# A two-block model on one core: the first block's state space steps laid between half tiles of its input projection

## The chip, the core and the metric

The kernel runs on one core of a Trainium2 chip. The metric is the device time in microseconds of one execution, the median of three. The engines are TensorE (PE, with its weight loads as PEld), VectorE (DVE), ScalarE (ACT), GpSimd (POOL) and SyncE (SP); the last two mainly start transfers here. They run on their own and meet at semaphores.

## The reference

All in float32, 512 tokens of width 1024. The first block, cut to what the change touches:

```python
mod = (silu(c) @ w_ada + b_ada).reshape(6, 1024)      # shift, scale, gate, twice
h = rmsnorm(x) * (1 + scale_m) + shift_m
proj = h @ w_in                                       # pool 512 | z 1024 | xbc 1536 | dt 16
y_pool = pool_mixer(proj[:, :512])                    # trailing means of 2, 4, 8, 16 tokens, one 128x128 product a group
conv = silu(conv4(xbc) + conv_b)                      # xs 1024 | b 256 | c 256
dt = softplus(dt_raw + dt_bias); a = dt * -exp(a_log) # 16 heads
a_cs = cumsum(a within a chunk of 128)                # 4 chunks
decay = exp(where(causal, a_cs[l] - a_cs[s], -inf))   # 16 heads x 4 chunks, 128x128 each
y_diag = (c @ b.T * decay) @ (xs * dt)
states = b.T @ (exp(a_cs[-1] - a_cs) * xs * dt)       # scanned over the chunks to h_prev
y = y_diag + exp(a_cs) * (c @ h_prev) + xs * d_skip
y_ssd = rmsnorm(y * silu(z)) * ssd_norm
x = x + gate_m * (concat([y_pool, y_ssd]) @ w_out)    # 1536 -> 1024
h = rmsnorm(x) * (1 + scale_f) + shift_f              # goes to the query product of a top-k expert layer
```

Behind it come the expert layer and a second block (gated linear attention, an S5 layer, a feed-forward part), which the change leaves as they are. The S5 layer's parameter tables are made early, in the shadow of the first block's output and query products.

## The kernel before, in words

Activations lie feature major: 8 regions of 128 features x 512 tokens in one large SBUF tile, `arena`. A product of the projection is a 128x128 weight tile against 128x512 tokens; 8 of them (12 in the output product) fill one PSUM bank, an output tile. `STAGES` names the stages: "in" has 24 tiles (12 of xbc, 8 of z, 4 of pool), "out" 8, "query" 16.

Order is what the code of each engine says. `Turn` (L163) issues an instruction and waits for its own semaphore before the next one, unless the name begins with "~". Semaphores of many events are shared (`SHARED`), so events of one semaphore must come in the order of that table. `bank_free` counts banks copied out of PSUM, `unit_done` counts finished weight tiles, and SP reloads a ring of four weight slots after them.

- POOL's queue loads the constants, c, w16 (the weights of dt), x, then 48 rows of w_ada through 8 buffers; a buffer is reused when VectorE has reduced its row (`mod_done`) and when the constants are there (`alone`).
- VectorE reduces 16 rows (`mod_row`), takes the reciprocal of the root, modulates x (`modulated`, two operations a tile), reduces 32 more rows, runs 12 convolutions (one multiply, three multiply-adds each), waits for the four pool tiles, pools them, then makes softplus on 16 partitions x 512 tokens and a scan.
- TensorE sums squares (L1218), makes dt (L1243) and all 24 tiles (`stage_products`, L521), waits until all are copied out, transposes, makes the chunk states (L1281), and goes through the heads: a row of the head (L1292, a selector of 16 partitions against the scan), which VectorE subtracts from the column (`seg`), ScalarE turns into a decay by Relu and Exp (`dec_e`), VectorE masks (`mdec`), and TensorE multiplies (`ssd_diag`, L1235). Two buffers alternate. After 8 heads come three products with the states (L1300) and the transposes back (L1226); then the gate with Silu(z).
- After 16 heads: one square of everything, sum of squares, root, norm (`ymix`), the four pool products (L1319), and only then the output product (L502), which waits for `pool_out` and `ymix` at its start. VectorE then makes the S5 tables and adds the tiles to x; the tables' products stand behind output tiles 4 to 7 (`tables_after`). The second norm and modulation repeat the pattern of the first, and the query product follows.

## Time and profile before

| | |
|---|---|
| median of three runs | 3052.07 us (3051.73 to 3059.96) |
| profiled execution | 3057.77 us, span 3056.1 us |
| TensorE busy | 2762.0 us (90%) |
| VectorE, ScalarE, POOL busy | 1880.7, 912.5, 868.6 us |
| chain that ended last | 60% TensorE, 16% issue, 16% VectorE |
| mean granted TensorE clock | 0.95 |

How it is read: "busy" is the time in which an instruction runs, not time at its peak. The clock row is the granted share of 2.4 GHz, so 0.50 is the lower level of 1.2 GHz. "Idle before" an instruction belongs to the event that released it. A float32 product appears as two matrix instructions, a transpose as one. The first block up to its query product takes the first 562 us of the span.

### The profile page before, as it was taken

The numbers are of one execution on the slowest core, as the hardware profiler recorded it, in microseconds if no ns is written. First come the engines' busy times: TensorE is split into PE (matmuls) and PEld (weight loads), VectorE is DVE, ScalarE is ACT, GpSimd is POOL, SyncE is SP. The second block draws the span as 40 slices with busy tenths as digits, with TensorE's granted clock in tenths as the row PEclk, the third lists the DMA queues.
The fourth block names the chain that finished last, engine by engine and source line by source line (L and its number), as shares of the span: only waits on it lengthen the run. The fifth ranks groups of instructions, "written<-read, shape, count | busy, mean of one in ns | idle before, by whom it ended". The sixth has DMA issues, their size and how long they took to land.

```text
span 3056.1 us, 36105 instructions
## 1 busy us (share of the span) xinstructions
PE 2762.0 (90%) x12753; PEld 2143.8 (70%) x12753; DVE 1880.7 (62%) x3290; ACT 912.5 (30%) x1121; POOL 868.6 (28%) x547
## 2 busy tenths in 40 slices
PE   4993769799996779999999999999999899899997
PEld 1442434348995569999999988779767777578875
DVE  7606356668999978888788889761114744361442
ACT  1020111223335643232332322344223323322221
POOL 3000000014660023344444432134212124244442
PEclk8995569899999999999999999999999999899999
DMA  8420003343332379989989889622713442222221
GB/s 335 160 87 9 0 33 108 127 155 104 118 121 119 154 262 317 317 306 323 316 309 317 302 299 319 211 90 82 140 42 102 138 146 90 69 83 96 91 96 62
DMA packets 190240, 500.79 MB, mean 164 GB/s; under 512 B 30704, under 2 KB 79872, under 8 KB 188080
## 3 DMA queue, kind: packets, MB, share of 16 engines
q1 hardware_dynamic: 140528, 315.20, 31.2%
q0 software_dynamic: 49616, 184.42, 16.8%
q8 instruction: 47, 0.77, 0.1%
q14 instruction: 49, 0.40, 0.0%
HBM read 452.70 MB, written 46.86 MB: 163 GB/s over the span
## 4 chain that ended last, share of the span: by engine, by line
PE 60%; issue 16%; DVE 16%; POOL 4%; DMA 1%; DVEq 1%; ACT 1%; POOLq 0%; ACTq 0%; SPq 0%
PE psum L1388 17%; PE psum L1670 13%; PE psum L1379 11%; PE psum L502 6%; PE psum L521 5%; DVE arena L1715 5%; POOL l_r L802 4%; DVE arena L1718 2%; DVE arena L1722 1%; PE psum L1292 1%; PE psum L1235 1%; DVE arena L2049 1%; DVE arena L2046 1%; DVE arena L2047 1%; DVEq L1718 1%
## 5 line engine op out<-in xcount | busy, mean ns | idle before, releaser
L827 ACT ACTIVATE arena<-psum 128x512 f32 (+7 forms) x487 | 328.3, 686 | 1282.9 <-PE psum L1379 392.6
L1715 DVE TENSOR_TENSOR arena<-arena 128x384 f32<-128x384 f32 (+11 forms) x396 | 342.0, 867 | 526.8 <-ACT arena L827 301.9
L802 POOL TENSOR_TENSOR l_r<-arena,l_r 128x1024 fp32r<-128x1024 f32 x144 | 352.2, 2447 | 704.8 <-ACT l_r L477 704.8
L1388 PE MATMUL psum<-e_r,e_r 128*128 128x512 f32 x2304 | 542.0, 392 | 11.1 <-DVE e_r L1715 11.1
L1379 PE MATMUL psum<-e_r,e_r 128*128 128x384 f32 x2048 | 524.7, 337 | 11.6 <-POOL l_r L774 8.0
L1388 PEld LDWEIGHTS psum<-e_r,e_r 128*128 128x128 f32 x2304 | 433.2, 189 | 99.7 <-issue 9.1
L1379 PEld LDWEIGHTS psum<-e_r,e_r 128*128 128x128 f32 x2048 | 369.7, 188 | 25.8 <-POOL l_r L774 15.0
L827 ACT ACTIVATE e_r<-arena 128x1024 fp32r<-128x1024 f32 x256 | 270.2, 1057 | 360.2 <-PE psum L1388 340.0
L1379 PE MATMUL psum<-e_r,l_r 128*128 128x384 f32 x1024 | 343.6, 336 | 0.0
L786 POOL DMA_INDIRECT arena<-in_down_rows,arena x128 | 162.8, 1272 | 424.4 <-DMA scratch_gates<-arena 179.7
L786 POOL DMA_INDIRECT arena<-in_up,arena x128 | 163.5, 1278 | 278.3 <-DVE arena L2145 144.3
L1715 DVE TENSOR_TENSOR e_r<-arena,e_r 128x384 fp32r<-128x384 f32 (+1 forms) x264 | 220.2, 877 | 13.4 <-ACT e_r L827 11.8
L502 PE MATMUL psum<-arena 128*128 128x512 f32 x448 | 199.8, 603 | 15.5 <-DVE arena L1719 14.6
L1722 DVE SCALAR_TENSOR_TENSOR arena<-arena 128x1024 f32<-128x1024 f32 (+5 forms) x157 | 191.5, 1221 | 24.7 <-ACT arena L827 15.2
L462 PE MATMUL psum<-p_r,l_r 128*128 128x264 f32 (+1 forms) x1024 | 196.1, 328 | 6.3 <-POOL l_r L802 5.2
L1670 PE MATMUL psum<-l_r,l_r 128*128 128x512 f32 x768 | 184.6, 401 | 11.0 <-DVE l_r L1722 11.0
L1379 PEld LDWEIGHTS psum<-e_r,l_r 128*128 128x128 f32 x1024 | 192.1, 188 | 0.0
L477 ACT ACTIVATE l_r<-arena 128x1024 fp32r<-128x1024 f32 x144 | 152.4, 1058 | 131.2 <-PE psum L1670 93.2
L1670 PE MATMUL psum<-f_r,l_r 128*128 128x512 f32 x768 | 181.8, 397 | 0.0
L1670 PEld LDWEIGHTS psum<-l_r,l_r 128*128 128x128 f32 x768 | 146.1, 191 | 49.6 <-issue 10.9
L1518 PE MATMUL psum<-p_r,l_r 128*128 128x512 f32 x576 | 179.2, 404 | 1.6 <-ACT arena L827 1.6
L462 PEld LDWEIGHTS psum<-p_r,l_r 128*128 128x128 f32 x1024 | 161.9, 190 | 25.2 <-issue 7.1
(222 smaller groups left out, 3435.7 us busy)
## 6 DMA issues: line engine op xcount, KB each, us to landing
arena<-in_down SPq DMA_DIRECT2D x128, 512.0 KB, 4.3
arena<-in_up SPq DMA_DIRECT2D x128, 512.0 KB, 6.6
arena<-in_w_ada POOLq DMA_DIRECT2D x48, 512.0 KB, 8.6
scratch_gates<-arena SPq DMA_DIRECT2D x12, 2048.0 KB, 6.3
arena<-scratch_gates SPq DMA_DIRECT2D x32, 768.0 KB, 9.8
arena<-in_w_in SPq DMA_DIRECT2D x44, 512.0 KB, 3.5
arena<-in_w_query SPq DMA_DIRECT2D x16, 512.0 KB, 3.5
arena<-in_w_glu SPq DMA_DIRECT2D x16, 512.0 KB, 3.5
```

What stands on the lines that cost most here:

```text
L462: last = nc.tensor.matmul(bank(2 * j + h, cw), rr(w_ + k * P, P, "l"), x_[:, c0:c0 + cw], start=(p == 0 and k == 0 and n == 0), stop=(p == ...
L502: last = nc.tensor.matmul(bank(2 * (v % 4)), wslot(s, kt)[:, k, :], rhs(k, 0, w), start=(k == 0), stop=(k == kt - 1))
L521: last = nc.tensor.matmul(bank(2 * j + h, cw), wslot(s, kt)[:, k, :], rhs(p * kt + k, c0, cw), start=(p == 0 and k == 0), stop=(p == parts ...
L786: pool.indirect_dma_start(reg(GATH + g % NGATH * 1024, 1024), None, rows_d if kind == "d" else rows_u, bass.IndirectOffsetOnAxis(reg(at_, ...
L802: nc.gpsimd.tensor_tensor(rr(lo, 1024, "l"), reg(RING + q % NSLOT * SLOT, 1024), rr(hi, 1024, "l").bitcast(F32), ALU.subtract).then_inc(S[ ...
L827: do(sc.activation(out, in_, f, **kw), sem)
L1379: last = mm(bank(b, TD), w__, rr(b_ + k * TD, TD), start=(k == 0 and n == 0), stop=(k == 7 and n == 2))
L1388: last = mm(bank(2 * tt_ + hf), rr(w__ + tt_ * P, P), rr(x__ + hf * 512, 512), start=(first and n == 0), stop=(final and n == 2))
L1518: last = mm(bank(v % 2), rr(w__ + k * P, P, "l"), x_[:, META:T2], start=(k == 0 and n == 0), stop=(k == 7 and n == 2))
L1670: last = mm(bank(2 * (t % 4)), rr(w__ + k * P, P, "l"), x_[:, META:T2], start=(p == 0 and k == 0 and n == 0), stop=(p == parts - 1 and k = ...
L1715: do(v.tensor_tensor(out, a, b, op), sem)
L1722: do(v.scalar_tensor_tensor(out, a, s, b, op0, op1), sem)
```

## The change

It rewrites the order of the first block.

- Loads: c and 8 rows of w_ada go first on POOL's queue and the constants behind them; SP loads x in 8 parts, and w_in's first four tiles after 6 rows are reduced. The order of w_in is now xbc, pool, z. X is overwritten by the chunk states and loaded again (`x_again`) before the output tiles are added to it.
- First norm: squares tile by tile, sum of squares tile by tile; VectorE multiplies by the reciprocal root (`scaled_x`), ScalarE applies scale and shift (`modulated`), and tile 0 starts with the first of them. The second norm (`xr2`, `h2_ready`) is built alike.
- Time steps token major: dt is 32 products with tokens on the output's partitions, softplus and the rest are on 128 x 64, the cumulative sum is a product with the causal matrix (`acol`), and a head's row is four products of a broadcast column of `a_col` with the same matrix (`ssd_row`). Selector and scan are gone. ScalarE takes the difference from the column as the bias of Relu, so VectorE's subtraction is gone.
- Convolutions: ScalarE makes the first tap while it copies; VectorE runs them between rows of w_ada, during the projection.
- Tiles 12 to 23 of the projection are cut into halves of four products (`in_half`), which stand between the state space steps. The pool tiles are pooled and multiplied among the first eight heads. Tiles 16 to 23 share bank 6.
- The first four products of output tiles 0 to 3 (the pool rows) are issued before the state space rows are ready; their other eight follow after the norm.

The diff, cut to its core ("..." where lines are left out):

```diff
-HST = H
-BTOK = H + 3072
+HST = X
+BTOK = X + 3072
...
+            if first:
+                for k in range(KT):
+                    sp.dma_start(reg(X + k * T, T), io["xT"][k * P:(k + 1) * P, :]).then_inc(S[f"x_in{k}"], 16)
+                sp.wait_ge(S["mod_done"], S.base("mod_done") + 6)
...
+        def in_bank(v):
+            return 2 * (v % 4) if v < 12 else 6 + v % 2 if v < 16 else 6
+        def in_free(v):
+            return v + 1 if v < 12 else 16 if v < 14 else v + 3 if v <= 16 else v + 4
+        def far_bank(v):
+            return (6, 2, 4, 0)[v % 4]
...
+            pool.dma_start(reg(CACT, D), io["c"].broadcast_to([P, D])).then_inc(S["c_in"], 16)
+            for m in range(8):
+                pool.dma_start(reg(ADA + m * 1024, 1024), io["w_ada"][m]).then_inc(S[f"ada_in{m}"], 16)
             pool.dma_start(cst[:, :], io["consts"]).then_inc(S["small_in"], 16)
...
+            def modulated(shift0, sem, done):
+                for k in range(KT):
+                    wait(sem, k + 1)
+                    h = reg(H + k * T, T)
+                    act_(h, h, ACT.Identity, "~" + done, scale=gsc[:, k:k + 1], bias=mod[:, shift0 + k:shift0 + k + 1])
...
+            def decay(h):
+                wait("row_mm", h + 1)
+                if h >= 2:
+                    wait("diag_mm", h - 1)
+                m = MB_ + (h % 2) * T
+                for c in range(NCH):
+                    act_(reg(m + c * P, P), bank(h % 2)[:, c * P:(c + 1) * P], ACT.Relu, FREE if c < 3 else None, scale=-1.0,
+                         bias=acol[:, c * 16 + h:c * 16 + h + 1])
+                act_(reg(m, T), reg(m, T), ACT.Exp, "~dec_e", scale=-1.0)
...
+            def ssd_row(h):
+                if h >= 2:
+                    w_("dec_e", h - 1)
+                for c in range(NCH):
+                    last = mm(bank(h % 2)[:, c * P:(c + 1) * P], bc(a_col[:, c * 16 + h:c * 16 + h + 1], [P, P]), causal,
+                              start=True, stop=True)
...
-            stage_products(pe, "in", tok(H))
-            drained("in")
+            for v in range(1, 12):
+                in_part(pe, v, 0, KT)
+                if v == 4:
+                    w_("a_col", 1)
...
+            ssd_xs(0)
+            ssd_xs(1)
+            in_half(13, 0)
+            ssd_xs(2)
+            ssd_xs(3)
+            in_half(13, 1)
+            w_("btok", 2)
+            ssd_state(0)
+            in_half(14, 0)
...
+            for h in range(8):
+                ssd_row(h)
+                in_half(16 + h // 2, h % 2)
+                if h:
+                    ssd_diag(h - 1)
+                if h >= 4:
+                    pool_mix(h - 4)
...
+            for v in range(4):
+                far_tile(pe, "out", v, YMIX, 4, 12, (lambda k: w_("ymix", k - 3)) if v == 0 else None)
+            for v in range(4, 8):
+                far_tile(pe, "out", v, YMIX, 0, 12)
+                tables_after("out", v)
...
-            for n in range(16):
+            for n in range(12):
+                mod_row(n)
+            wait("small_in", 48)
+            tt(g_sq, pr("norm_final"), pr("norm_final"), ALU.mult)
+            ts(g_sq, g_sq, EPS, None, ALU.add, sem="g_sq")
+            wait("rt1", 1)
+            do(v.reciprocal(RS[:, 0:T], RS[:, 0:T]))
+            for n in range(12, 16):
                 mod_row(n)
```

How the instructions stand now. First VectorE at the end of the first norm; L1744 and L1930 reduce a row of w_ada, L1754 and L1939 are the reciprocal. Before:

```order
L1744 ISA arena,mod<-arena 128x1024 [waits ada_in7,mod_done]
L1744 ISA mod 128x1
L1715 TENSOR_TENSOR mod<-mod,par 128x16 [waits mod_done]
L1722 SCALAR_TENSOR_TENSOR gsc<-mod,par 128x8 [waits dve_own]
L1754 RECIPROCAL rs<-rs 128x512 [waits act_events,dve_own]
```

And after:

```order
L1904 TENSOR_TENSOR gsc<-par 128x8 [waits small_in,mod_done]
L1908 TENSOR_SCALAR gsc<-gsc 128x8 [waits dve_own]
L1939 RECIPROCAL rs<-rs 128x512 [waits act_events,g_sq]
L1930 ISA arena,mod<-arena 128x1024 [waits ada_in4,dve_own]
L1930 ISA mod 128x1
L1930 ISA arena,mod<-arena 128x1024 [waits ada_in5,mod_done]
L1930 ISA mod 128x1
L1930 ISA arena,mod<-arena 128x1024 [waits ada_in6,mod_done]
L1930 ISA mod 128x1
L1930 ISA arena,mod<-arena 128x1024 [waits ada_in7,mod_done]
L1930 ISA mod 128x1
L1904 TENSOR_TENSOR mod<-mod,par 128x16 [waits mod_done]
```

The reciprocal has moved ahead of four rows, and it now stands behind the wait for the constants (`small_in`).

TensorE in the first heads; L1292 and L1342 make a head's row, L1235 and L1333 are the masked products, L519 is a half tile. Before:

```order
L1281 MATMUL psum<-arena 128x512 x6
L1292 MATMUL psum<-rs,arena 128x512 x2
L1235 MATMUL psum<-arena 128x64 x4
L1292 MATMUL psum<-rs,arena 128x512
L1235 MATMUL psum<-arena 128x64 x4
L1292 MATMUL psum<-rs,arena 128x512
```

And after:

```order
L519 MATMUL psum<-arena 128x512 x8
L1342 MATMUL psum<-cst,small 128x128 x4
L519 MATMUL psum<-arena 128x512 x4
L1342 MATMUL psum<-cst,small 128x128 x4
L519 MATMUL psum<-arena 128x512 x4
L1333 MATMUL psum<-arena 128x64 x4
L1342 MATMUL psum<-cst,small 128x128 x4
L519 MATMUL psum<-arena 128x512 x4
```

Between a head's row and its masked products now stand two half tiles and the next row, where one row stood.

TensorE at the start of the output product; L502 and L534 are its tiles, L1218 and L1386 sums of squares, L1319 the pool products, L1300 and L1364 the products with the states. Before:

```order
L1300 MATMUL psum<-arena 128x512 x3
L1226 MATMUL psum<-cst,arena 128x128 x16
L1218 MATMUL psum<-arena,cst 128x512 x8
L1319 MATMUL psum<-arena 128x512 x4
L502 MATMUL psum<-arena 128x512 x60
L1226 MATMUL psum<-cst,arena 128x128 x8
```

And after:

```order
L1364 MATMUL psum<-arena 128x512 x3
L534 MATMUL psum<-arena 128x512 x4
L1323 MATMUL psum<-cst,arena 128x128 x12
L534 MATMUL psum<-arena 128x512 x4
L1323 MATMUL psum<-cst,arena 128x128 x4
L1386 MATMUL psum<-arena,cst 128x512 x4
L534 MATMUL psum<-arena 128x512 x4
L1386 MATMUL psum<-arena,cst 128x512 x4
L534 MATMUL psum<-arena 128x512 x48
L1323 MATMUL psum<-cst,arena 128x128 x8
```

Four groups of four output products have moved ahead of and between the transposes and the sum of squares, and the pool products are gone from here.

## Rows read from the trace of the kernel before

**Rows 1.** Windows: span, length, busy of PE PEld DVE ACT POOL, granted clock, DMA share, GB/s

```profile
4.00:48.00 44.00, 9.40 (x16) 3.88 (x16) 27.33 (x43) 8.04 (x6) 13.26 (x25) 0.84 1.02 401
...
62.66:227.70 165.04, 165.04 (x385) 72.87 (x384) 64.25 (x105) 25.55 (x38) 11.30 (x21) 1.00 0.40 147
227.70:262.06 34.36, 0.03 (x2) 0.03 (x1) 29.02 (x48) 3.34 (x5) 0.00 (x0) 0.56 0.07 23
262.06:299.68 37.62, 22.62 (x78) 13.81 (x78) 18.06 (x28) 2.35 (x7) 0.00 (x0) 0.64 0.00 0
299.68:413.37 113.69, 82.78 (x204) 45.54 (x204) 41.45 (x62) 20.15 (x32) 0.00 (x0) 0.50 0.00 0
413.37:443.71 30.34, 15.66 (x25) 5.96 (x25) 12.01 (x14) 7.04 (x5) 1.07 (x2) 0.67 0.19 72
443.71:533.67 89.96, 89.96 (x240) 41.55 (x240) 60.02 (x98) 12.51 (x20) 4.45 (x7) 0.98 0.27 91
533.67:562.15 28.48, 9.25 (x17) 3.73 (x17) 12.29 (x18) 6.45 (x5) 0.50 (x1) 0.72 0.05 16
...
227.70:232.00 4.30, 0.02 (x1) 0.00 (x0) 3.31 (x6) 0.60 (x1) 0.00 (x0) 1.00 0.53 183
232.00:236.00 4.00, 0.00 (x0) 0.00 (x0) 3.73 (x9) 0.00 (x0) 0.00 (x0) 0.50 0.00 0
```

**Rows 2.** Timeline of TensorE: start, busy us, engine, line, operation, shapes [idle before <-releaser]

```profile
22.57 9.40 PE L1218 MATMUL psum<-arena,cst 128*128 128x512 f32 x16 [22.57 <-ACT arena L827]
53.51 9.21 PE L1243 MATMUL psum<-arena,w 128*16 128x512 f32 x16 [21.54 <-DVE arena L1719]
...
310.19 1.97 PE L1235 MATMUL psum<-arena 128*128 128x64 f32 x8 [1.38 <-DVE arena L1715]
312.09 2.07 PE L1292 MATMUL psum<-rs,arena 16*128 16x512 f32 x2
...
496.95 1.04 PE L1226 MATMUL psum<-cst,arena 128*128 128x128 f32 x8
...
562.15 16.15 PE L502 MATMUL psum<-arena 128*128 128x512 f32 x32 [14.57 <-DVE arena L1719]
...
693.59 6.64 PE L1368 MATMUL psum<-arena 128*128 128x128 f32 x58
```

**Rows 3.** Timeline of VectorE, prologue to output stage

```profile
13.43 0.17 DVE L1715 TENSOR_TENSOR gsc<-par 128x8 f32<-128x8 f32 x1 [10.87 <-DMA w<-in_w]
...
20.17 1.23 DVE L1744 CUSTOM_DVE_ANT_0 arena<-arena 128x1024 f32<-128x1024 f32 x1 [6.37 <-DMA arena<-in_w_ada]
...
41.01 3.35 DVE L1754 RECIPROCAL rs<-rs 128x512 f32<-128x512 f32 x1
...
100.03 2.33 DVE L1722 SCALAR_TENSOR_TENSOR arena<-arena,par 128x512 f32<-128x512 f32 x3
...
314.20 0.69 DVE L1715 TENSOR_TENSOR arena<-psum,small 128x512 f32<-128x512 f32 x1 [4.06 <-PE psum L1292]
...
457.24 2.56 DVE L1715 TENSOR_TENSOR arena<-arena 128x64 f32<-128x64 f32 x10
...
473.04 1.41 DVE L1722 SCALAR_TENSOR_TENSOR arena<-psum,mod,arena 128x512 f32<-128x512 f32 x2
...
487.52 5.00 DVE L1715 TENSOR_TENSOR arena<-arena 128x1024 f32<-128x1024 f32 x4
```

**Rows 4.** Timeline of ScalarE, in the same stages

```profile
201.16 9.01 ACT L827 ACTIVATE arena<-arena,par 128x512 f32<-128x512 f32 x12 [0.18 <-ACT arena L827]
...
309.63 1.29 ACT L827 ACTIVATE arena<-arena 128x512 f32<-128x512 f32 x2 [4.06 <-DVE arena L1715]
...
413.37 3.62 ACT L827 ACTIVATE arena<-arena 128x4096 f32<-128x4096 f32 x1 [18.85 <-DVE arena L1715]
...
428.57 0.60 ACT L827 ACTIVATE rs<-psum 128x512 f32<-128x512 f32 x1
436.03 1.28 ACT L827 ACT_TABLE_LOAD   x1 [6.86 <-DMA arena<-in_s5a]
```

## What I predicted, before the changed kernel ran

> **What bounds the kernel now.** The page's busy shares say TensorE is at 90%, but the windows by stage show where it isn't. I read these first [rows 1]. From 62.66 us TensorE is full for 165.04 us (24 tiles of the input projection; each product is two of the 385 instructions of 0.43 us, so 0.86 us for a product of 128x512 and 6.88 us for a tile). Then it stands still for 34.36 us (pooling and time steps on VectorE), is busy 22.62 of 37.62 us, 82.78 of 113.69 us (the 16 heads) and 15.66 of 30.34 us, and all of this at a granted clock of 0.50 to 0.67, half of it at the 1.2 GHz level. The output product is full again (89.96 us), the second norm costs 28.48 us, then the query product starts at 562.15. The timelines show why [rows 2 to 4]: one head is a ring. TensorE makes a row (2.07 us at half clock), VectorE subtracts (0.69, after waiting 4.06), ScalarE does Relu and Exp (1.29), VectorE masks, TensorE multiplies. No engine has other work in it. So the path to 562.15 is: prologue, projection, vector work alone, ring, norm, output, norm. What comes after is not touched.
>
> **What the change does to the sum.** Zero is the span's start; I follow TensorE in the new order, at full clock where it has work.
>
> Prologue. c and the first 8 rows of w_ada now go first on POOL's queue, x on SP's, w_in only after 6 modulation rows. DMA moves 401 GB/s [rows 1]. Before, w16 had landed at 13.43 [rows 3]; 1.74 MB of POOL's and as much of SP's were ahead, 8.7 us, so 4.7 us go to start and completion. By that, w_ada row 0 lands at about 10 instead of 20.17 [rows 3], but the constants, behind 4.7 MB on POOL's queue and 2.1 MB of x, land at about 24.5 instead of 13.4. Two things are queued behind that: TensorE's sum of squares and POOL's loads of w_ada from row 8 on. The first takes 9.40 us [rows 2], to 34, its root 0.60 [rows 4], the table being loaded already. Row 8 needs issue, transfer and completion, so it comes at about 30, and the next every 1.3 us (0.52 MB at 401 GB/s). VectorE needs 1.28 us a row [rows 3], so 12 rows end at 35.5, the reciprocal (3.35, [rows 3]) at 39.4, four rows at 44.5, the first product with x at 45.6 (0.69 to 0.72), ScalarE's scale and shift at 46.4 (0.75, [rows 4]). Tile 0 starts there; its 8 products find TensorE as long idle as the 8 of the time steps did at 53.51, and take their 9.2 us [rows 2]: 55.7. The time steps become 32 products of 16 columns. No row has this form. Bounds: 0.13 us each (transposes, 1.04 for 8) and 0.29 us (9.21 for 32, the old cost); I take the 0.229 of 128-column products (6.64 for 29, [rows 2]), since each loads 128x128 weights: 7.3 us. **Tile 1 starts at 63.0** instead of 69.5.
>
> Tiles 1 to 12. 11 x 6.88 and two small products: 138.9. VectorE in that time: rows 16 to 25, softplus now on 128x64 instead of 16x512 (24 operations of about 0.26, [rows 3], 6 us), then 12 times a convolution (2.33, [rows 3]) and two rows: ends 142.6, 2.4 us after the last tile is copied out; its Silu 143.5. Tile 12 waits for the last copy-out (0.9) and ends at 146.7, so it covers this, with 3 us to spare. The pooling and softplus stretch of 34.36 us is gone from the path.
>
> Transposes, states. 8 + 32 transposes and 8 products of 128 columns 7.1 us, 6 products of 512 columns 5.2, six halves of tiles 13 to 15 20.6, two gaps of 0.95 where a half tile does not stand between two transposed chunks: 34.8, so **181.5**. The halves cover xdt, xdte and the state updates (0.7 to 2.8 us each against 3.44).
>
> Heads. A head now costs TensorE 0.92 (four row products at 0.229) + 3.44 (half tile) + 0.92 (four mask products). The first eight, with four pool products of 0.86, are 44.7 us: 226.2. The mask of a head is wanted 7.8 us after its row. ScalarE needs four Relu of 128 columns, which no row shows: between 0.15 us each (a quarter of a 128x512 from PSUM, 0.60) and 0.60. A square of 4096 columns took 3.62, so 512 columns beyond the first cost 0.45 and 0.15 is fixed [rows 4]: 0.15 + 0.11, and I take 0.3. With Exp that is 1.9 us, at worst 3.1; the mask adds 0.7. At both ends it is hidden; if the cover were gone it would cost about 3 us a head. The bank of tiles 16 to 23 is one, so each waits for its predecessor's copy-out, 0.8 us against 1.9 of other products: hidden. The second eight with 8 halves, 3 state products, 16 transposes and two stalls (1.6 for the last token row, 2.0 for the last mask) are 51.4: **277.6**.
>
> To the output product. 3 state products 2.6, four first halves of output tiles (pool rows) 13.7, transposes 2.1, sum of squares 6.9: 302.9, with the sum ending at 299.4. Root, reciprocal and first scaled row then take 5.1 us (0.6 + 3.35 + 0.75 and hand-overs), of which 3.44 is hidden: 304.5. Second halves 27.5: 332.0, tile 4: 342.3. x is loaded a second time after 280 on POOL's queue, 2.1 MB, which by the count above takes 10 us, and is wanted at 339; S5's parameters stand behind it on that queue, but are issued only at 299.4.
>
> What is late next: VectorE. Its tables start when S5's parameters land, 8.8 us after the sum of squares (Exp's table load at 436.03 against the root at 428.57 after its own 1.28 load, [rows 4]), at 310. To the first output tile it took 29.3 us (443.7 to 473.04, [rows 1, 3]), 2.9 for four output tiles, 3.75 for the first table product (three of the four in 5.00): 346.0. Before, the output product was 53 us in by then; now TensorE has done half of it ahead and is at 342.3. It waits 3.7. The rest, at full clock: tables 5.7, tiles 5 to 7 31.0, third sum of squares 6.9, none of it waited for: **389.4**.
>
> Second norm. Before 28.48 us, with one square of 4096 columns ahead (3.62, [rows 4]) and all eight rows of modulation behind the reciprocal. Now squares are made tile by tile, the shift is on ScalarE: root 0.8, reciprocal 3.35, one row 0.7, one scale 0.9: 5.8 us. **The query starts at 395.2** instead of 562.15, with the same cold 2.2 us as before (16.15 for 16 products that take 13.9 at full clock, [rows 2]).
>
> The sum: 562.15 - 395.2 = 167 us. By piece: 6.5 at tile 1; from there to the stretch of pure output product 374.2 us before (69.5 to 443.7), now 241.5 (to 304.5), 132.7 less with 13.7 us of output product already in it; from there to the query 118.4 before, now 90.7, 27.7 less. The profiled execution took 3057.77 us (span 3056.1): 2891. It lies 5.7 us above the median of the runs, 3052.07, and the runs spread 8; I take **2888**.
>
> **Clock.** Everything above takes the 2.4 GHz level from tile 1 on. The rows: the clock fell to 0.50 4.3 us after TensorE stopped at 227.7 [rows 1]; through the heads, 73% busy with gaps of 1.4 us, it stayed at 0.50; with output tiles and bursts of transposes back to back it was 0.98. The new stretch is over 95% busy, with no gap over 2 us. The wait of 3.7 us may cost a restart, 2.2 us. The Trainium skill (TensorE: Matmul & The Clock Gate, "A second HAM failure mode: psum-queue depth-cycling") says that a kernel changing banks often idles so briefly and often between groups that the clock swings. The trace has such a stretch, the heads, but with 27% idle. By the page's rule the new stretch would partly run at half clock, which is the first rival.
>
> **Rivals.**
> (1) The clock stays low or swings between tile 12 and the end of the state space steps. Their 153 us hold about 147 us of products. If the 35 us of transposes and states alone run at half, +30: 2918; if all do, +147: 3035. For: many small products, each with a wait that may come late. Against: busy share. Chance 0.08.
> (2) The same mechanism, up to the query: some 239 us of products lie between tile 12 and 395, and all at half clock cost 239 us less the 10 or so of stalls they hide: 3117, **slower than before**. It decides at about 70% of that work (166 of 239 us). The rows at 0.98 in the output product, which is unchanged there, speak against it. Chance 0.01.
> (3) VectorE and DMA bind more than I count. Constants as late as 30 us, tables 10 us later, convolutions past tile 12: 15 to 30 us: 2903 to 2918. For: the 3 us of margin at the convolutions and the 3.7 already lost. Against: VectorE's 60 us of work in the output stage [rows 1] have 79 us there. Chance 0.17.
> (4) The change doesn't overlap what it says: TensorE takes instructions in order, so a half tile stands behind a late mask. With no cover each head pays its 3 us: +48, 2936. Against: 4.9 us of slack. Chance 0.03.
> My forecast, 2870 to 2902: 0.71.
>
> **How the numbers follow.** Below: time steps at 0.13 (-3), no stalls at all (-12), spread of runs: 2870. Above: to 2925, which holds rival (3) and the small form of (1) and leaves out some 0.1. A measurement tells 0.3% (9 us) from no change; all cases but (2) and a tail of (1) are faster: 0.97 faster, 0.01 the same, 0.02 slower.
>
> **What would show it.** Tile 1 near 63; TensorE over 93% busy from there to the output product, at a clock of 0.95 or more; no gap over 1 us between heads; VectorE released by TensorE's rows nowhere; a wait of TensorE for VectorE after output tile 4 of 2 to 6 us; query from 390 to 405; all after it alike, shifted. It is wrong if the clock row shows 5 in the stretch, if the constants land after 30, or if the query's own stage changes length.

## The result, and the profile after

The changed kernel takes **2907.84 us** (median of four runs, 2900.84 to 2908.74) against 3053.58 for the kernel before in the same session: a ratio of 0.951 [0.950, 0.952], 146 us less. The forecast was 2888 with a range of 2870 to 2925 and 0.97 for faster. So the direction and the range held, and the gain fell 21 us short of the 167 us of the sum. The profiled execution took 2908.15 us with a span of 2906.5. The query product, up to which the sum went, starts at 411.02 us instead of 562.15; I had forecast 395.2. What follows the query takes 2495.5 us, 1.5 more than before: the shortfall lies ahead of it.

The page of the changed kernel, engines and their 40 slices:

```profile
PE 2709.8 (93%) x12891; PEld 2136.9 (74%) x12891; DVE 1847.6 (64%) x3241; ACT 949.3 (33%) x1223; POOL 869.1 (30%) x546
...
PE   4999899999877899999999999999998999899997
...
PEclk8999999999999999999999999999999999899999
```

The clock row has no slice below 0.8, and in TensorE's row the first block, its first six slices, has no digit below 8 behind the prologue. The same is in the windows of the changed kernel, cut at the starts of its stages: start:end, length, busy of PE PEld DVE ACT POOL, granted clock, DMA share, GB/s. In order: tile 0, time step products, tiles 1 to 11, tile 12 up to the heads, heads, states and first output halves, second halves and tile 4, rest of the output product.

```profile
46.34:54.75 8.41, 8.40 (x17) 3.75 (x17) 8.27 (x15) 4.81 (x7) 1.59 (x3) 0.82 0.54 189
54.75:63.89 9.14, 9.14 (x65) 9.14 (x64) 4.67 (x8) 1.32 (x2) 2.65 (x5) 0.76 0.94 354
63.89:143.81 79.92, 79.14 (x181) 34.90 (x182) 60.20 (x107) 23.03 (x39) 9.26 (x17) 0.96 0.54 183
143.81:189.32 45.51, 41.22 (x132) 21.05 (x133) 19.80 (x34) 5.44 (x9) 0.00 (x0) 0.96 0.15 52
189.32:284.27 94.95, 91.66 (x415) 57.07 (x414) 36.18 (x57) 41.21 (x95) 0.00 (x0) 1.00 0.18 61
284.27:312.60 28.33, 26.85 (x72) 12.38 (x71) 14.47 (x18) 8.19 (x12) 2.01 (x3) 0.94 0.34 112
312.60:361.29 48.69, 40.24 (x89) 17.48 (x89) 44.32 (x83) 10.96 (x16) 0.87 (x1) 0.89 0.27 96
361.29:411.02 49.73, 43.80 (x137) 20.95 (x136) 25.14 (x26) 11.78 (x21) 4.48 (x7) 0.97 0.29 101
```

Against the forecast, stage by stage:

| stage | forecast, us | measured, us | difference |
|---|---|---|---|
| to tile 0 | 46.4 | 46.34 | 0 |
| tile 0 and time steps (to tile 1) | 16.6 | 17.55 | +0.9 |
| tiles 1 to 11 (to tile 12) | 76.8 | 79.92 | +3.1 |
| tile 12, transposes, states | 41.7 | 45.51 | +3.8 |
| sixteen heads | 96.1 | 94.95 | -1.2 |
| states, first output halves, norm | 26.9 | 28.33 | +1.4 |
| second halves, tile 4 | 41.5 | 48.69 | +7.2 |
| tiles 5 to 7, second norm | 49.2 | 49.73 | +0.5 |

Before, the stretch that these heads replace took 113.69 us with 82.78 of TensorE at a clock of 0.50 [rows 1]; now the sixteen heads, with sixteen half tiles (eight whole tiles) and the four pool products among them, take 94.95, at 1.00. Five rows of TensorE's timeline show what is left: start, busy, instruction, count, and in brackets the idle time ahead and what ended it.

```profile
54.75 9.30 PE L1395 MATMUL psum<-w,arena 128*128 128x16 f32 x64
...
168.67 3.65 PE L1359 MATMUL psum<-arena 128*128 128x512 f32 x4 [2.33 <-DVE arena L1904]
...
312.60 27.73 PE L534 MATMUL psum<-arena 128*128 128x512 f32 x64 [1.49 <-DVE arena L1911]
348.78 12.67 PE L534 MATMUL psum<-arena 128*128 128x512 f32 x24 [8.45 <-DVE arena L1911]
...
411.02 14.42 PE L534 MATMUL psum<-arena 128*128 128x512 f32 x29 [5.93 <-ACT arena L859]
```

Between 168.67 and 312.60 the only waits of TensorE are 1.51 us at 250.85 and 1.78 at 283.33. The largest one, 8.45 us, stands ahead of output tile 4. What VectorE did in that time, from its timeline:

```profile
318.53 0.48 DVE L1904 TENSOR_TENSOR arena<-arena 128x64 f32<-128x64 f32 x2 [1.35 <-ACT arena L859]
...
340.33 7.52 DVE L1904 TENSOR_TENSOR arena<-arena 128x1024 f32<-128x1024 f32 x6
347.88 2.73 DVE L1911 SCALAR_TENSOR_TENSOR arena<-psum,mod,arena 128x512 f32<-128x512 f32 x4
350.53 5.00 DVE L1904 TENSOR_TENSOR arena<-arena 128x1024 f32<-128x1024 f32 x4
```

The S5 tables fill it from 318.53 to 347.88; only then does it add output tile 0 to x (347.88) and free that tile's PSUM bank. Tile 4 uses the same bank, and starts 0.90 us later.

### The profile page after: what moved, and what is told of

It reads as the page before. It is cut to its first block, busy times and chain, and to the rows that moved or that the text cites. A ratio compares the mean times of both kernels' runs of the same rounds, so it can differ in the third digit from the quotient of the medians.

```text
span 2906.5 us, 36296 instructions
## 1 busy us (share of the span) xinstructions
PE 2709.8 (93%) x12891; PEld 2136.9 (74%) x12891; DVE 1847.6 (64%) x3241; ACT 949.3 (33%) x1223; POOL 869.1 (30%) x546
## 4 chain that ended last, share of the span: by engine, by line
PE 60%; issue 17%; DVE 14%; POOL 5%; DMA 2%; DVEq 1%; ACT 1%; POOLq 0%; ACTq 0%; SPq 0%
PE psum L1577 18%; PE psum L1859 14%; PE psum L1568 11%; PE psum L534 6%; PE psum L519 6%; POOL l_r L834 4%; DVE arena L1904 4%; DVE arena L1907 2%; DVE arena L2254 1%; DVE arena L2251 1%; DVE arena L2252 1%; DVEq L1907 1%; DVE arena L2250 1%; DVE arena L2253 1%; DVE arena L1911 1%
## 5 line engine op out<-in xcount | busy, mean ns | idle before, releaser
L1904 DVE TENSOR_TENSOR arena<-arena 128x384 f32<-128x384 f32 (+8 forms) x394 | 340.3, 868 | 489.8 <-ACT arena L859 270.7
L1568 PEld LDWEIGHTS psum<-e_r,e_r 128*128 128x128 f32 x2048 | 369.6, 188 | 25.9 <-POOL l_r L806 14.9
L534 PE MATMUL psum<-arena 128*128 128x512 f32 x448 | 200.7, 604 | 15.9 <-DVE arena L1911 9.9
L1911 DVE SCALAR_TENSOR_TENSOR arena<-arena 128x1024 f32<-128x1024 f32 (+5 forms) x157 | 191.4, 1220 | 24.7 <-ACT arena L859 15.2
L519 PE MATMUL psum<-arena 128*128 128x512 f32 x384 | 173.6, 605 | 13.8 <-ACT arena L859 13.8
```

The lines of the kernel that those rows point to most:

```text
L519: last = nc.tensor.matmul(bank(in_bank(v)), wslot(s, KT)[:, k, :], A[:, H + k * T:H + (k + 1) * T], start=(k == 0), stop=(k == KT - 1))
L534: last = nc.tensor.matmul(bank(far_bank(v)), wslot(s, kt)[:, k, :], A[:, src + k * T:src + (k + 1) * T], start=(k == 0), stop=(k == kt - 1))
L1568: last = mm(bank(b, TD), w__, rr(b_ + k * TD, TD), start=(k == 0 and n == 0), stop=(k == 7 and n == 2))
L1904: do(v.tensor_tensor(out, a, b, op), sem)
L1911: do(v.scalar_tensor_tensor(out, a, s, b, op0, op1), sem)
```

## The experiments

They are compared by two things: the median of the runs, and the profiled execution cut at three marks, tile 12's start, the first head's row, and the query product's start. From tile 12 to the query the changed kernel takes **267.2 us** (45.5 + 95.0 + 126.8). The stretch from tile 0 to tile 12 is told apart, since it varies from run to run (below). The medians alone are too coarse for most of these edits: the runs of one kernel lie up to 13 us apart (2893.61 to 2906.98 in experiment 7), and what follows the query, which no edit touches, takes between 2490.0 and 2498.7 us in the profiled executions. Two short starts behind a wait, at full clock in some executions and at half in others, also move the stretch from tile 12 on by 1.7 us each (last section).

**1. Is TensorE the bound in the heads, or the ring?** All of tiles 16 to 23 ahead of the heads, as whole tiles, in two banks in turn and with their copies out of PSUM ahead of the heads as well:

```diff
             for h in range(8):
                 ssd_row(h)
-                in_half(16 + h // 2, h % 2)
...
+            for v in range(16, 24):
+                in_half(v, 0)
+                in_half(v, 1)
+            for h in range(8):
+                ssd_row(h)
```

> The changed kernel with one part undone: tiles 16 to 23 of the projection are no longer cut up between the heads but stand as whole tiles ahead of them (two banks in turn). Same products, same work of every engine. In the changed kernel the query product starts at 411.0 us. My theory: the half tiles hide a ring of row, Relu and Exp, mask and masked product. Without them two heads cost 0.83 + 0.92 + 1.9 + 0.8 and hand-overs, some 4.8 us, the first four heads 3.8 us each for pooling on VectorE, so the 16 heads take 46 to 50 us where TensorE has 28 us of its own: 18 to 22 us later if the clock stays at the upper level, up to 42 us later if it falls to 0.50 with the gaps. Rival 1 (the gain came from the shorter ring and the token major steps alone, the cover does nothing): within 3 us of 411.0. Rival 2 (in the changed kernel single-bank tiles cost as much as they hide): faster.

2937.91 us, ratio 0.961 [0.959, 0.963]. Tile 12 to the query took 298.3 us, 31 more than with the halves in between. Waits of 0.8 to 3.1 us stand before the mask and state products, and a window over the heads shows the clock lower too:

```profile
230.00:330.00 100.00, 81.48 (x358) 58.50 (x357) 40.91 (x66) 41.01 (x93) 0.91 (x1) 0.81 0.12 38
```

Against a clock of 1.00 and 91.66 of 94.95 us in the changed kernel. So laying half tiles between the heads is worth 31 us of the gain, by cover and clock together. It is not the whole of it: with the heads uncovered the kernel is still 117 us faster than before.

**2. How much cover do the heads need?** Tiles 16 to 23 with two of their eight products, the rest left out (six of the eight terms of z are missing from the sum):

```diff
-                in_part(pe, v, 4 * hf, 4 * hf + 4)
+                if v < 16:
+                    in_part(pe, v, 4 * hf, 4 * hf + 4)
+                elif hf == 0:
+                    in_part(pe, v, 0, 1)
+                else:
+                    in_part(pe, v, 7, 8)
```

> The changed kernel with work left out: tiles 16 to 23 (z) make only 2 of their 8 products, one in each half, so z is wrong and the time is that of a shorter cover. 48 products of 0.86 us are gone, 41.3 us. Theory (TensorE's own work sets the heads, the ring has some 4.9 us of slack a head): the query starts 30 to 41 us earlier than 411.0, that is at 370 to 381; the 8 to 11 us missing are the first four heads, where VectorE pools. If the ring or ScalarE's queue set the pace of the heads already, less than 10 us come off.

2876.45 us, ratio 0.941 [0.940, 0.943]. Tile 12 to the query took 235.3 us, 31.9 less; in the heads alone 66.66 us instead of 94.95, 28.3 less for 41.3 us of products taken away. Six waits more than in the changed kernel come up there, of 0.47 to 1.73 us, 7.5 us together, and the clock is 0.95: TensorE is busy 56.05 us, where 50.4 would be left of 91.66. So with a full half tile per head TensorE's work is what sets the time, and with a quarter of one the ring shows again. The other 3.6 us lie outside the heads; 3.4 of them are two starts after a wait that here were not at half clock (1.96 instead of 3.65, 2.79 instead of 4.49).

**3. The fall of the clock ahead of tile 1.** In the changed kernel the windows show 0.50 from 60 to 68 us, with TensorE busy in every one of them. The suspect is the run of 32 products of 16 columns. First, the same products in four groups of 8 between quarters of tile 1:

```diff
             for c in range(NCH):
+                in_part(pe, 1, 2 * c, 2 * c + 2)
                 for k in range(KT):
...
-            for v in range(1, 12):
+            for v in range(2, 12):
```

> The changed kernel with one move: the 32 products of 16 columns for the time steps no longer stand in a row after tile 0, but in four groups of eight, each behind two products of tile 1. In the changed kernel the granted clock went from 1.00 at 58 us to 0.50 by 60 and back to 1.00 only at 70, with TensorE busy all the time. Theory (a run of products with few columns lets the clock fall, whatever busy says): the clock stays at 1.00 in 52 to 75, tile 2 starts 3.5 to 4.5 us earlier, and so does everything to the wait before output tile 4. Rival (the clock falls there because of the cold start or by chance): it falls in the same place, nothing changes. VectorE's softplus comes at the same time, since ScalarE's part of it already stands behind tile 1.

2899.37 us, ratio 0.949 [0.947, 0.950]. The windows of this kernel and, beneath, of the one of experiment 6, where the run of 32 is left as it was:

```profile
60.00:70.00 10.00, 10.00 (x58) 7.13 (x57) 0.00 (x0) 1.10 (x2) 0.53 (x1) 1.00 0.65 258
70.00:80.00 10.00, 10.00 (x28) 4.74 (x28) 8.45 (x29) 3.55 (x7) 1.06 (x2) 1.00 0.62 196
```

```profile
62.00:66.00 4.00, 4.00 (x21) 4.00 (x20) 0.00 (x0) 0.00 (x0) 0.00 (x0) 0.50 1.03 418
66.00:70.00 4.00, 4.00 (x14) 3.06 (x14) 1.42 (x3) 0.00 (x0) 0.00 (x0) 0.50 0.35 136
70.00:74.00 4.00, 4.00 (x6) 1.69 (x5) 1.27 (x4) 0.00 (x0) 1.05 (x2) 0.52 0.45 140
```

In groups, tile 0 to tile 12 takes 94.05 us; in one run it takes 97.47 in the changed kernel, and between 95.96 and 100.65 in the other kernels that keep it. A group of 8 takes 1.70 us from its start to the next instruction, 0.21 a product. This comparison hides a part of the fall, since the clock happened to rise earlier in the changed kernel's tile 0: from 50 to 52 us its clock was 1.00, that of the kernel with groups still 0.50, and tile 0 took 8.4 us against 10.0. From the end of tile 0 to tile 12 it is 89.06 us against 84.1 (tile 0's end in the kernel with groups taken two products, 1.7 us, ahead of the first group). In the nine kernels with the long run this stretch is 87.4 us three times, 89.1 three times and 90.7 three times: the fall costs 3.3, 5.0 or 6.6 us, and 5.0 in the changed kernel.

Then the run by itself, away from its place. To the kernel with the groups, 32 products were added behind tile 7, where the clock has long been at 1.00, into an unused bank; their result is read by nobody. Once they are of 16 columns, once of 128:

```diff
+                if v == 7:
+                    for c in range(NCH):
+                        for k in range(KT):
+                            mm(bank(3)[:, 0:16], reg(H + k * T + c * CH, CH), w16[:, 0:16], start=(k == 0), stop=(k == 7))
```

> The kernel with the time step products in four groups, and behind tile 7 another 32 products of 16 columns into an unused bank, whose result nothing reads: work added. Theory, that a run of narrow products itself lowers the granted clock while TensorE stays busy: a slice of 0.50 to 0.6 within or just behind the run, and tile 0 to tile 12 takes 94 + 9 to 15 = 103 to 109 us. Rival, that the fall belongs to the place after tile 0 (transfers, VectorE's steps): the clock stays 1.00 and the run costs 32 x 0.21 = 6.7 us, tile 0 to tile 12 about 101.

> The same with 32 added products of 128 columns in place of the 16 columns, at the same place, whose result nothing reads: work added. Theory, that narrowness is what lowers the clock: the clock stays 1.00 there and the run costs 32 x 0.23 = 7.3 us, tile 0 to tile 12 about 101.5. Rival, that any run of short products lowers it: a slice at 0.50 to 0.6 here too, and 105 us or more.

2912.96 us (2909.97 to 2914.93; 0.953 [0.952, 0.955]) with 16 columns, 2907.88 (2907.01 to 2908.99; 0.952 [0.950, 0.953]) with 128: no run of the one is as short as any of the other. Windows, first of the 16 columns, whose run goes from 113.16 to 121.90, then of the 128 columns, from 110.89 to 118.03:

```profile
116.00:118.00 2.00, 2.00 (x21) 2.00 (x20) 1.97 (x3) 0.00 (x0) 0.51 (x1) 1.00 0.43 172
118.00:120.00 2.00, 2.00 (x14) 2.00 (x13) 1.89 (x5) 0.00 (x0) 0.55 (x2) 0.59 0.61 180
120.00:122.00 2.00, 2.00 (x11) 2.00 (x11) 1.93 (x4) 0.00 (x0) 0.00 (x0) 0.50 0.84 211
122.00:124.00 2.00, 2.00 (x4) 0.97 (x4) 1.01 (x2) 0.00 (x0) 0.00 (x0) 0.50 0.33 133
124.00:126.00 2.00, 2.00 (x4) 0.81 (x4) 0.00 (x0) 0.00 (x0) 0.00 (x0) 0.70 0.00 0
```

```profile
114.00:116.00 2.00, 2.00 (x20) 2.00 (x19) 1.93 (x5) 0.00 (x0) 0.53 (x1) 1.00 0.14 55
116.00:118.00 2.00, 2.00 (x20) 2.00 (x19) 1.93 (x3) 0.00 (x0) 0.53 (x1) 1.00 0.73 236
118.00:120.00 2.00, 2.00 (x7) 0.98 (x7) 1.93 (x4) 0.00 (x0) 0.00 (x0) 1.00 0.77 193
```

Same place, same count, TensorE and its weight loads as busy, with VectorE and transfers at work in both: 16 columns bring the clock down, 128 columns don't. Tile 0 to tile 12 took 104.41 and 100.22 us; from the start of tile 2 it is 80.61 against 77.28, so with eight times the columns the stretch is 3.3 us shorter. That this fall belonged to the place after tile 0 is ruled out.

**4. The wait of 2.33 us ahead of the first states.** Its product needs `btok` and `xdte`, and I had it ready. The trace has VectorE's last masks of the chunk products end at 168.5, and the states start at 168.67:

```profile
163.83 3.50 DVE L1904 TENSOR_TENSOR arena<-arena,small 128x1024 f32<-128x1024 f32 x3
167.24 1.28 DVE L1904 TENSOR_TENSOR arena<-psum,cst 128x512 f32<-128x512 f32 x2
```

The first row is `xdte` of three chunks, of which the first is ready at about 165.0; the second is the masks. TensorE stood from 166.3 on. `hst` shares a semaphore of many events with those, so the wait for a region that is still free counts them too. Without that wait for the first chunk, which needs none:

```diff
-                w_("hst", 2 * c)
+                if c:
+                    w_("hst", 2 * c)
```

> The changed kernel without one wait: the first state products no longer wait for count zero of the state updates. That count shares its semaphore with the masks of c and b (cbm), so waiting for zero means waiting for both masks. The banks written are free by another wait (btok). In the changed kernel TensorE idled 2.33 us there and the clock fell to 0.50 for 3 us. Theory: the idle time falls to 0 to 0.5 us (xdte is ready at 165.1, TensorE at 166.3), the clock stays up, the heads start 3 to 4 us earlier than 189.3. Rival (xdte itself is late): no change.

2901.33 us, ratio 0.950 [0.949, 0.952]; tile 12 to the query 262.9, 4.3 less, all of it ahead of the heads. The row of TensorE's timeline:

```profile
165.69 1.88 PE L1360 MATMUL psum<-arena 128*128 128x512 f32 x4
```

No wait, and 1.88 us where it took 3.65: 2.3 us of the 4.3 is the wait and 1.7 the slow start behind it. The 1.7 is not there in every execution: four other kernels, with the same wait of 2.33 us, took 1.95 or 1.96 (last section).

**5. What the output halves are worth.** Halves of tiles 1 to 3 put back behind the norm; tile 0's four pool products stay ahead of it, behind the sum of squares:

```diff
-            far_tile(pe, "out", 1, YMIX, 0, 4)
             w_("yt_ready", 5)
...
-                far_tile(pe, "out", v, YMIX, 4, 12, (lambda k: w_("ymix", k - 3)) if v == 0 else None)
+                far_tile(pe, "out", v, YMIX, 0, 12, (lambda k: w_("ymix", k - 3) if k > 3 else None) if v == 0 else None)
```

> The changed kernel with the part on the output product mostly undone: the first four products of output tiles 0 to 3 no longer stand before and between the transposes and the sum of squares; tile 0's four stand behind the sum, those of tiles 1 to 3 behind the norm. Theory: VectorE's chain of S5 tables starts with the sum of squares' end (parameters are loaded then), and it, not the norm, is what TensorE waits for later. The sum ends 6.9 to 10 us earlier, so out tile 4's bank is free 7 to 10 us earlier; TensorE idles about 2 us more at the norm and none (instead of 8.45) before tile 4: the query starts 3 to 8 us EARLIER than 411.0. Rival (what the change says: pool rows hide the norm): about 5 us later, since 3.4 more of the norm's wait is exposed and the start of the cold clock with it.

2898.43 us, ratio 0.949 [0.947, 0.951]. Tile 12 to the query takes 256.6, 10.7 less. Two starts after a wait were at full clock here and not in the changed kernel, 1.7 us each; 7.3 us remain, near the upper end of the 3 to 8 that I expected. This part of the change, as it is placed, loses time. The timeline tells why:

```profile
288.84 1.53 PE L1323 MATMUL psum<-cst,arena 128*128 128x128 f32 x12 [2.44 <-DVE arena L1900]
...
291.55 7.03 PE L1386 MATMUL psum<-arena,cst 128*128 128x512 f32 x16
298.42 3.60 PE L534 MATMUL psum<-arena 128*128 128x512 f32 x8
303.50 48.33 PE L534 MATMUL psum<-arena 128*128 128x512 f32 x112 [1.49 <-DVE arena L1907]
```

The sum of squares ends 14.9 us after the state products begin (at 283.61), against 23.4 in the changed kernel, which has two halves ahead of it and one in its middle. Root, S5's transfer and all of VectorE's tables hang on that sum. With them 8.5 us earlier, and 48.33 us of products without a break instead of 27.73, the tables are off the path: no wait ahead of tile 4 is left. It costs waits of 2.44 and 0.69 us at the transposes.

**6. Tile 4 in another bank.** Bank 5 is free there, so tile 4 need not wait for tile 0's addition:

```diff
+        def out_bank(v):
+            return 5 if v == 4 else far_bank(v)
...
-                pe.wait_ge(S["bank_free"], S.base("bank_free") + tiles[name] + v + 1)
+                pe.wait_ge(S["bank_free"], S.base("bank_free") + tiles[name] + v + (0 if name == "out" and v == 4 else 1))
```

> The changed kernel with output tile 4 in the free bank 5 instead of bank 6, so that it doesn't wait for VectorE to add tile 0 to x, which VectorE does only behind 29 us of S5 tables. In the changed kernel TensorE idled 8.45 us there and ran cold after it. Theory: tile 4 starts at 340.3 instead of 348.8 and runs warm; then the table product after it waits for VectorE (354.4 by its rows: 348.0 + 2.7 + 3.75) about 4 us: it starts 6 to 7 us earlier than 361.3, and the query too, at 404 to 405.5. Rival (VectorE is the bound of the whole stage, so a moved wait comes back in full): query within 1.5 us of 411.0.

2896.51 us, ratio 0.948 [0.946, 0.950]. Tile 12 to the query 262.8, 4.4 less:

```profile
316.80 38.03 PE L538 MATMUL psum<-arena 128*128 128x512 f32 x88 [1.49 <-DVE arena L1915]
358.21 1.97 PE L1327 MATMUL psum<-cst,arena 128*128 128x128 f32 x8 [3.38 <-DVE arena L1908]
359.97 12.47 PE L538 MATMUL psum<-arena 128*128 128x512 f32 x24
```

This is the order of my forecast, and here its numbers come out: the wait stands at the table product and is 3.38 us (3.7 forecast). The table product starts 210.2 us after tile 12 instead of 217.5, 7.3 sooner. Of that 2.9 are lost again, because the products behind the wait run at half clock for a while (1.97 and 12.47 us against 1.04 and 10.46). So the query came 4.4 us sooner by this count, not the 6 to 7 that I expected; the rival, that the wait comes back in full, had at most 1.5.

**7. The sum of squares ahead of the halves.** Halves of tiles 1 and 2 moved behind all eight products of the sum:

```diff
-            far_tile(pe, "out", 1, YMIX, 0, 4)
             w_("yt_ready", 5)
             ssd_back(7, 1)
-            for k in range(4):
+            for k in range(8):
                 square_tok(H, 7, "sq2", k, "ss2")
+            far_tile(pe, "out", 1, YMIX, 0, 4)
             far_tile(pe, "out", 2, YMIX, 0, 4)
```

> The changed kernel with the sum of squares of the state space norm ahead of the first halves of output tiles 1 and 2 instead of between and behind them; all first halves stay ahead of the norm's end. Theory (the S5 chain on VectorE starts with that sum and binds the output stage): the sum ends about 5.5 us earlier (302 instead of 307.5), the wait for the norm disappears, the wait before output tile 4 shrinks from 8.45 by about 4 us, the query starts 4 to 6 us earlier than 411.0. Rival (the order of the halves does nothing once they are all ahead of the norm): within 1 us.

2900.87 us, ratio 0.949 [0.947, 0.950]; tile 12 to the query 260.7, 6.5 less. The norm's wait of 1.49 is gone, as two more halves cover it, and the wait ahead of tile 4 is 3.25 instead of 8.45:

```profile
299.37 7.03 PE L1386 MATMUL psum<-arena,cst 128*128 128x512 f32 x16
306.23 37.93 PE L534 MATMUL psum<-arena 128*128 128x512 f32 x88
347.42 12.23 PE L534 MATMUL psum<-arena 128*128 128x512 f32 x24 [3.25 <-DVE arena L1909]
```

That is near what taking the halves out brought (7.3): it is not the halves that cost time but their place ahead of the sum.

**8. The prologue.** The constants behind four rows of w_ada instead of eight, and w_in after ten rows:

```diff
-            for m in range(8):
+            for m in range(4):
                 pool.dma_start(reg(ADA + m * 1024, 1024), io["w_ada"][m]).then_inc(S[f"ada_in{m}"], 16)
...
-                sp.wait_ge(S["mod_done"], S.base("mod_done") + 6)
+                sp.wait_ge(S["mod_done"], S.base("mod_done") + 10)
```

> The changed kernel with another order of loads: constants, w16 and dtal go behind the first 4 rows of w_ada instead of behind 8, and w_in's first tiles are asked for after 10 modulation rows instead of 6. In the changed kernel VectorE idled 7.66 us before row 8, since POOL asks for it only when the constants are in. Theory (the constants' place makes that gap): constants in at about 19.5 instead of 23.7, no gap at row 8, tile 0 starts at 41.5 to 43.5 instead of 46.3, tile 1 as much earlier. Rival (the bytes bind, 401 GB/s whatever the order): tile 0 within 1 us of 46.3. If w_in then comes too late, tile 0 waits for it instead.

2899.25 us, ratio 0.949 [0.947, 0.950]. The constants are there at 19.66 instead of 23.66, tile 0 starts at 43.03 instead of 46.34; the stages from there to the query are the same to 0.1 us. VectorE's gap ahead of row 8, 7.66 us before, is gone; one of 3.90 us ahead of row 4 stands in its place, and twelve rows end 3.3 us sooner (31.99 against 35.29). What the later start of w_in gave by itself was not measured apart.

**9. All of it in one kernel**, with small moves more: a half of tiles 12 to 15 between every two transposed chunks, row 10 and tile 23's second half one step over, one S5 table made under the second norm. And the changed kernel once more beside it.

> Everything that the single edits showed, in one kernel, with four small edits more: no wait for the Relu's ring before the first states (4.3 us in its run), the time step products in four groups inside tile 1 (3.4), the constants behind four rows (3.3), tile 4's output in another bank with the sums of squares ahead of the output halves (4.4 and 6.5, part of them the same time: together 8 to 12), halves of tiles 12 to 15 between all transposed chunks (1 to 2), tile 23's second half after row 15 (about 1.5), tokens one row earlier (about 1), one table built earlier (1 to 2). Theory, that these are separate waits on TensorE's own path: the query product starts between 382 and 388 us, the median is 2880 (2874 to 2887). Rival, that a wait taken away comes back at the next ring or as a lower granted clock: the query product starts between 392 and 400, the median is 2890 to 2896.

> The changed kernel again, beside the others on one chip: 2901 to 2908 us, the query product between 408 and 414, and the stretch from tile 12's start to the query product 266 to 268.5 us. The stretch from tile 0 to tile 12 moves with the length of the fall of the granted clock: 96 to 101 us.

**2873.03 us** (2871.8 to 2877.8, five runs), ratio 0.940 [0.939, 0.942]; the changed kernel 2907.14 (2900.57 to 2910.23), 0.951 [0.950, 0.952], with 267.1 us from tile 12 to the query, as before. That is 34 us less than the changed kernel and better than either theory gave. Its windows, cut at tile 0, tile 12, inside the heads, at the first output half and at the query:

```profile
42.43:134.83 92.40, 91.62 (x260) 44.63 (x261) 73.11 (x129) 29.22 (x48) 13.44 (x25) 0.98 0.65 225
134.83:199.24 64.41, 64.23 (x245) 36.02 (x245) 34.87 (x61) 17.25 (x38) 0.00 (x0) 1.00 0.19 62
199.24:268.78 69.54, 68.93 (x311) 42.81 (x311) 23.18 (x34) 31.05 (x67) 0.00 (x0) 1.00 0.19 61
268.78:377.39 108.61, 103.91 (x289) 48.66 (x288) 81.60 (x122) 29.16 (x48) 6.94 (x11) 1.00 0.35 119
```

From tile 12 to the query it takes 242.6 us, 24.7 less: 6.3 ahead of the heads, 2.9 in them, 15.5 behind. The parts had shown 4.3, nothing, and 4.4 and 6.5 by themselves. Another 3.9 us lie ahead of tile 0, and 5.1 between it and tile 12 (92.40 against 97.46). The rest is partly clock, since no wait over 0.7 us is left between tile 12's start and the second norm, and none is followed by a slow start. The second norm's wait is 4.01 instead of 5.93, as a table product now covers part of it. Which of the small moves gave how much of the remaining few microseconds was not measured apart.

## Why the prediction was right, and where it fell short

**Right: the prologue.** Every step of it came within a microsecond or so: constants at 23.66 (24.5), row 8 at 30.23 (30), tile 0 at 46.34 (46.4). The bandwidth argument held.

**Right: the heads.** 94.95 us against 96.1, at clock 1.00, with waits of 1.51 and 1.78 (1.6 and 2.0 forecast). The bounded term, four Relu of 128 columns, is in ScalarE's timeline:

```profile
194.74 1.14 ACT L859 ACTIVATE arena<-psum,small 128x128 f32<-128x128 f32 x4 [1.24 <-PE psum L1342]
195.92 0.63 ACT L859 ACTIVATE arena<-arena 128x512 f32<-128x512 f32 x1
```

1.14 us for four, 0.285 each (0.3 taken). Rivals (1), (2) and (4) fell with it. Experiment 1 shows that what I called hidden is hidden by the half tiles; its price without them, 31 us, was below the 48 of rival (4), where I had put 3 us on every head.

**Right: what hangs on VectorE.** From the first table operation to output tile 0 it took 29.35 us (29.3 forecast); the norm's wait was 1.49 (1.6), the second norm's 5.93 (5.8).

**Wrong: the wait ahead of tile 4, +7.2 us.** "332.0, tile 4: 342.3" let tile 4 follow the second halves at once and put the only wait behind it, at the table product. Tile 4 has tile 0's bank, and that is free only when VectorE has come through its tables. I had priced VectorE's order rightly and asked it of one reader only. So tile 4's 10.3 us stand behind the wait instead of beside it, and another 2.2 went to their slow start (12.67 us against 10.46 for the same 24 instructions). Experiment 6, which takes away the bank alone, gives the forecast's own order and wait.

**Wrong in its sign: the output halves.** The sum counted them as cover for the norm, 3.44 us. They cover it, but three of the four stand ahead of the sum of squares or in it, and the tables behind that sum were the next thing late. The forecast itself had a wait for VectorE there, so each of the microseconds by which the sum came later should have been weighed against it. Experiments 5 and 7 put 6.5 to 7.3 us on that place.

**Wrong: the step to the heads, +3.8 us.** "The halves cover xdt, xdte and the state updates" was right of the data and left out the semaphore. The wait of 2.33 was for an event that the product doesn't need; with it went 1.7 us of slow start. Experiment 4 gives back 4.3.

**Wrong: the clock behind tile 0, 5.0 us.** "Everything above takes the 2.4 GHz level from tile 1 on." I looked for idle time as the cause of a low clock, as the rows of before showed it [rows 1]. The run of narrow products is not idle for a moment, and the clock fell in it. Experiment 3 shows that it is the run's narrowness. The sizes of the sum were right: it has 84.1 us from tile 0's end to tile 12 (7.3 and 76.8), the kernel with groups took 84.1, the changed kernel 89.06. In the table these 5.0 us are the +3.1 and the +0.9, the latter with 0.8 taken off, since tile 0 took 8.4 us and not 9.2.

Rival (3), that VectorE binds more, is what happened, by its smaller end (15.8 us at the query against its 15 to 30), but with other terms: neither the constants nor the convolutions were late. About 10.6 us, the greater part of the 15.8, are slow stretches of the clock: 5.0 at the narrow run, 1.7 each at the first states and at the six behind the last mask, 2.2 at tile 4. I had named a restart of 2.2 us behind the wait for VectorE and left it out of the sum.

Of the rest of the distance to 2888, 1.5 us came behind the query, and the other 2.7 are the step from the profiled execution to the median. The sum gave 2891 by the profile of before, which lay 5.7 above its median, and I took 3 off. The profiled execution of after lay on its median (2908.15 and 2907.84). One slip of adding is in the sum: from 346.0 its terms 5.7, 31.0 and 6.9 give 389.6, not 389.4.

**The signs.** These held: tile 1 near 63 (63.89), TensorE 96% busy from there to the output product at a mean clock of 0.97, no wait of VectorE for a head's row, the constants before 30, no 5 in the clock row. These did not: the query starts at 411.02 (390 to 405 forecast), the wait for VectorE stands ahead of output tile 4 and is 8.45 us (2 to 6, behind it), and two waits in the heads are over 1 us, which the sum itself had. The clock row was too coarse for a sign: each of its slices is 73 us long, and the fall at 60 to 68 us shows only in windows of a few microseconds.

## What to carry to other kernels

When a late engine is found, ask for every resource that its delayed instructions give back, PSUM banks and shared semaphores too, and let the first reader of any of them wait, not the one that reads the result. Work moved forward as cover belongs behind the instruction on which the longest chain of another engine hangs, not ahead of it. A wait of two microseconds costs more than itself where TensorE restarts at the lower clock, so taking several out together can bring more than their sum.

## What the hardware did that I had not expected

**The granted clock fell with TensorE busy without a gap.** In each of the nine kernels with 32 float32 products of 16 columns in a row behind tile 0, and in the tenth with them behind tile 7, the profiled execution has a stretch of about 7, 10 or 14 us at 0.50 that begins within the run; with 8 in a row, or 32 of 128 columns, there was none. Where it came, it cost between 3.3 and 6.6 us (experiment 3), so it alone spreads the times of otherwise equal kernels by 3.3 us. The Trainium skill (TensorE: Matmul & The Clock Gate, "Part 1: The HAM clock gate") says that the gate goes by how busy TensorE has been of late. Busy time as the profile has it doesn't bear that out: 2.00 of 2.00 us in both runs, and the clock fell in one. Whether the array itself counts as less busy with 16 columns no view here shows.

**A wait of some two microseconds is a coin toss for the clock.** The four instructions behind the 2.33 us wait took 1.95 or 1.96 us in four of the kernels and 3.57 to 3.65 in seven, with the same wait and the same instructions just ahead; the six behind the 1.78 us wait took 2.79 in three kernels and 4.49 in eight. In the combined kernel, with waits of 0.7 us and less, they took 1.88 and 2.79.
